# A two-layer streaming encoder: constants loaded later, attention probabilities and values as half-precision pairs, the norm's steps in another order

## The reference

```python
z = x @ w_in[l] + b_in[l]
...
kv = (ckv_all @ w_ukv[l]).reshape(B, past + T, MLA_HEADS, NOPE_DIM + V_DIM)
a_out = _mla_attention(qn, qr, positions, kv[..., :NOPE_DIM], kr_all, kv[..., NOPE_DIM:], kpos)
...
h, C, n, m = _mlstm(mq, mk, mv, mi, mf, C_init, n_init, m_init)
...
c_out, v_rows = _gmlp(gu, gv, gmlp_ln_g[l], gmlp_ln_b[l], gmlp_ws[l], gmlp_bs[l])
...
x = _layernorm(DN_ALPHA * x + merged @ w_out[l], ln1_g[l], ln1_b[l])
moe_out = _moe(x, router_w, router_b, moe_w_gate[l], moe_w_up[l], moe_w_down[l],
               shared_w_gate[l], shared_w_up[l], shared_w_down[l])
x = _layernorm(DN_ALPHA * x + moe_out, ln2_g[l], ln2_b[l])
```

```python
s = jnp.einsum('bqhd,bkhd->bhqk', qn, kn) + jnp.einsum('bqhd,bkd->bhqk', qr, kr)
...
p = jax.nn.softmax(s, axis=-1)
return jnp.einsum('bhqk,bkhd->bqhd', p.astype(v.dtype), v)
```

## Time and profile before

| | |
|---|---|
| median of 3 runs | 1021.45 us (1021.13 to 1022.71) |
| profiled execution, own time | 1021.76 us |
| its span, first to last instruction | 1019.9 us |
| PE busy | 979.0 us (96%) |
| PEld (weight loads, beside PE) | 757.6 us (74%) |
| DVE busy | 806.5 us (79%) |
| ACT busy | 655.3 us (64%) |
| DMA | 205.02 MB, mean 201 GB/s |
| mean granted TensorE clock | 0.993 of full |

### The profile page before, as it was taken

The page is one execution under the profiler, slowest core; times in us unless marked ns, Lnnn a source line. Parts: engine busy times, 40 slices in busy tenths (PEclk is TensorE's granted clock), DMA queues, the critical chain, the costliest instruction groups (busy, mean ns, idle before and its releaser), DMA issues.

```text
span 1019.9 us, 24037 instructions
## 1 busy us (share of the span) xinstructions
PE 979.0 (96%) x9862; PEld 757.6 (74%) x9862; DVE 806.5 (79%) x1436; ACT 655.3 (64%) x1057; POOL 0.7 (0%) x10
## 2 busy tenths in 40 slices
PE   8999999999999999999999999999999989999995
PEld 6877777777776799976568777777777768998653
DVE  4796767654689899998888876676448899999986
ACT  5675454754355799876776645556543659987864
POOL 0000000000000000000000000000000000000000
PEclk9999999999999999999999999999999999999998
DMA  9845454423465199998836534442334435999961
GB/s 352 301 170 166 148 151 121 131 83 110 145 222 166 54 322 368 360 361 317 288 125 210 181 124 141 151 146 85 104 124 148 144 102 167 359 364 365 375 233 55
DMA packets 59652, 205.02 MB, mean 201 GB/s; under 512 B 7216, under 2 KB 10348, under 8 KB 59020
## 3 DMA queue, kind: packets, MB, share of 16 engines
q1 hardware_dynamic: 55980, 195.95, 55.8%
q10 hardware_dynamic: 3552, 7.42, 2.1%
HBM read 198.76 MB, written 3.40 MB: 198 GB/s over the span
## 4 chain that ended last, share of the span: by engine, by line
PE 64%; DVE 21%; DVEq 5%; ACT 4%; issue 3%; DMA 1%; SPq 1%; ACTq 0%
PE bank L1777 37%; DVE wlo L1074 12%; PE bank L1801 4%; DVEq L1700 4%; PE bank L2313 3%; ACT whi L555 2%; PE bank L2145 2%; PE bank L1806 1%; PE bank L2000 1%; DMA w<-in_w 1%; DVE mo L1702 1%; PE bank L2034 1%; PE bank L2076 1%; DVE xT L1087 1%; PE bank L2329 1%
## 5 line engine op out<-in xcount | busy, mean ns | idle before, releaser
L1074 DVE SCALAR_TENSOR_TENSOR wlo<-w,whi 128x1024 f16<-128x1024 f32 x358 | 428.9, 1220 | 69.4 <-ACT whi L555 67.9
L555 ACT ACTIVATE whi<-w 128x1024 f16<-128x1024 f32 x358 | 368.8, 1048 | 81.6 <-PE bank L1777 48.1
L1777 PE MATMUL bank<-xhi,whi 128*128 128x320 f16 x688 | 206.2, 300 | 0.7 <-DVE wlo L1074 0.6
L1777 PE MATMUL bank<-xhi,wlo 128*128 128x320 f16 x688 | 205.7, 299 | 0.0
L1777 PE MATMUL bank<-xlo,whi 128*128 128x320 f16 x688 | 205.7, 299 | 0.0
L1777 PE MATMUL bank<-arena_b,whi 128*128 128x112 f16 x2048 | 161.7, 213 | 7.7 <-DVE wlo L1074 6.7
L1777 PEld LDWEIGHTS bank<-arena_b,whi 128*128 128x128 f16 x2048 | 149.5, 98 | 12.8 <-issue 8.6
L1777 PE MATMUL bank<-arena_b,wlo 128*128 128x112 f16 x1024 | 157.3, 213 | 0.0
L1777 PEld LDWEIGHTS bank<-arena_b,wlo 128*128 128x128 f16 x1024 | 100.1, 98 | 0.0
L1777 PEld LDWEIGHTS bank<-xhi,whi 128*128 128x128 f16 x688 | 67.2, 98 | 30.8 <-issue 2.8
L1777 PEld LDWEIGHTS bank<-xhi,wlo 128*128 128x128 f16 x688 | 67.3, 98 | 26.1
(11 more groups left out here) (378 smaller groups left out, 1747.4 us busy)
## 6 DMA issues: line engine op xcount, KB each, us to landing
w<-in_w SPq DMA_DIRECT2D x358, 512.0 KB, 4.9
arena_b<-head_rows ACTq DMA_DIRECT2D x2, 1920.0 KB, 7.3
xT<-in_x SPq DMA_DIRECT2D x2, 640.0 KB, 5.5
out_y<-xT SPq DMA_DIRECT2D x4, 320.0 KB
rows<-in_rows ACTq DMA_DIRECT2D x1, 1024.0 KB, 10.5
rows<-in_rows SPq DMA_DIRECT2D x1, 1024.0 KB, 5.9
out_ckv<-arena_a SPq DMA_DIRECT2D x2, 320.0 KB
acc<-kr SPq DMA_DIRECT2D x2, 288.0 KB
```

The lines of the kernel that those rows point to most:

```text
L555: A(whi[:, n % SLOTS, :], w32[:, n % RAW, :], ACT.Copy, scale=WS).then_inc(hi_done.sem, 1)
L1074: V.scalar_tensor_tensor(wlo[:, n % SLOTS, :], w32[:, n % RAW, :], WS, whi[:, n % SLOTS, :], ALU.mult, ALU.subtract).then_inc(lo_done.sem, 1)
L1777: ins = M(out, w[:, s, sub * P:(sub + 1) * P], rhs(part, k), start=(n == 0), stop=(n == 3 * len(subs) - 1))
```

## The change

**Start.** Four constants (`ident`, `scan_keep`, `m_init`, `mats16`) stay ahead of block 4. `front_load` (mask, cosine, sine and the head rows) follows block 8, `head_load` (the five tables that ScalarE issued) block 10, and `router_load` (router weights, selection tables and biases) a block of the heads. Two new signals, `tables_in` and `router_in`, are waited for where the tables are used. The exponentials of the head rows and their store stand one block earlier on ScalarE.

**Attention.** The values are kept as two f16 parts (`v_hl`: high by ScalarE, low by VectorE). The exponential is written to one buffer `prob`; ScalarE multiplies it by 4096 over the sum into a high f16 part, VectorE writes the low one (`probs_lo`). The transposes are f16 matmuls of both parts with an identity, six a unit. Their result is again split in two (`columns_hi`, `columns_lo`), and the values are three f16 products each in place of one f32. On TensorE a unit is now scores, filler, values of the unit two before, transposes of the unit before. ScalarE and VectorE take the columns of the unit two before at the start of a unit. The second half's keys are copied out in two parts around unit 2's exponentials, its queries stand in unit 1.

**Norms.** The base `acc` is filled chunk by chunk as each merged chunk has been split, and the router's high part before it. In the first norm the square of residual 6 is added before the last product is waited for, no longer behind residual 7. In `ln_vector` one chunk is centred before the variance and the other seven within the loop, with four drains in it instead of two.

The diff, cut; renamed waits and declarations are left out:

```diff
             sp.dma_start(par[:, :], d["par"]).then_inc(par_in.sem, 16)
-            for dst, name in ((ident[:, :], "ident"), (mmask[:, :], "mmask"),
-                              (scan_keep[:, :], "scan_keep"), (mats16[:, :, :], "mats16"),
...
+            for dst, name in ((ident[:, :], "ident"), (scan_keep[:, :], "scan_keep"), (m_init[:, :], "m_init"),
+                              (mats16[:, :, :], "mats16")):
                 sp.dma_start(dst, d[name]).then_inc(consts_in.sem, 16)
...
+                for dst, name in ((mmask[:, :], "mmask"), (cosT[:, :], "cos"), (sinT[:, :], "sin")):
+                    sp.dma_start(dst, d[name]).then_inc(tables_in.sem, 16)
+                sp.dma_start(rows[:, :], d["rows"][0:1, :].broadcast_to([P, 4 * GW])).then_inc(rows_fr.sem, 16)
...
+            def head_load():
+                for dst, src in ((cache, d["cache"][0:P, :]), (kr[:, 0:PAST], d["krope"][0:ROPE, :]),
...
+            def router_load():
...
+                if n == RAW:
+                    front_load()
+                if n == RAW + 2:
+                    head_load()
+                if n == M0 + RAW:
+                    router_load()
...
-                if l == 0:
-                    act.dma_start(rows[:, :], d["rows"][0:1, :].broadcast_to([P, 4 * GW])
-                                  ).then_inc(rows_fr.sem, 16)
-                for dst, src in () if l else ((cache, d["cache"][bass.ds(l * P, P), :]),
...
+                    if i == 1:
+                        act.wait_ge(r_arg.sem, r_arg.value(l, 1))
+                        A(r_x[:, 1:4, :], r_x[:, 1:4, :], ACT.Exp).then_inc(r_exp.sem, 1)
...
+                def k_out(hf, parts=range(4)):
+                    for n in parts:
...
                 def exps(u):
                     act.wait_ge(s_max.sem, s_max.value(l, u + 1))
+                    if u:
+                        act.wait_ge(p_lo.sem, p_lo.value(l, u))
...
+                def probs_hi(u):
+                    act.wait_ge(p_inv.sem, p_inv.value(l, u + 1))
                     if u >= 2:
...
+                        A(prob_h[:, u % 2, 0, 0:P], prob[:, 0:P], ACT.Copy, scale=sm[:, 6:7])
+                        A(prob_h[:, u % 2, 0, P:3 * P], prob[:, P:3 * P], ACT.Copy, scale=sm[:, 7:8]
+                          ).then_inc(p_hi.sem, 1)
...
+                def columns_hi(u):
...
+                        A(prob_t[:, u % 2, 0, :], bank[6][:, 0:3 * P], ACT.Copy).then_inc(t_hi.sem, 1)
...
-                    A(br_hi[:, p * T:(p + 1) * T], bank[7][:, 0:T], ACT.Copy, scale=XS
+                    A(br_hi[:, p * T:(p + 1) * T], bank[7][:, 0:T], ACT.Copy, scale=1 / PS
...
                 for u in range(UNITS):
+                    if u >= 2:
+                        columns_hi(u - 2)
+                    if u == 2:
+                        k_out(1, (0, 1))
...
+                    if u == 4:
+                        v_out_hi(1)
+                    elif u not in (2, 3):
+                        gate_tanh(FILLER[u - 1] if u else 2)
+                    exps(u)
                     if u == 2:
-                        q_out(1)
-                    elif u == 3:
-                        k_out(1)
-                    elif u != 4:
-                        gate_tanh(FILLER[u - 1] if u else 2)
-                    if u:
-                        probs_out(u - 1)
-                    exps(u)
+                        k_out(1, (2, 3))
                     if u != 3:
                         hi_a(FILLER[u])
+                    if u == 1:
+                        q_out(1)
+                    probs_hi(u)
+                columns_hi(UNITS - 2)
                 gate_tanh(13)
                 hi_a(14)
                 gate_tanh(14)
-                probs_out(UNITS - 1)
+                columns_hi(UNITS - 1)
...
+                act.wait_ge(router_in.sem, 16 * 6)
+                A(rw_hi[:, :, :], rw[:, :, :], ACT.Copy, scale=WS).then_inc(rw_h.sem, 1)
+                for c in range(KD):
+                    act.wait_ge(m_lo.sem, m_lo.value(l, c + 1))
+                    if l:
                         a = A(acc[:, c * T:(c + 1) * T], xT[:, c * T:(c + 1) * T], ACT.Identity,
...
-                else:
-                    A(acc[:, :], xT[:, :], ACT.Copy, scale=ALPHA).then_inc(acc_pre.sem, 1)
...
+                    else:
+                        a = A(acc[:, c * T:(c + 1) * T], xT[:, c * T:(c + 1) * T], ACT.Copy, scale=ALPHA)
+                a.then_inc(acc_pre.sem, 1)
...
-                for c in range(2):
-                    centred(c)
+                centred(0)
...
-                centred(2)
+                dve.drain()
                 dve.wait_ge(ln_std.sem, ln_std.value(l, k + 1))
                 for c in range(KD):
-                    if c in (2, 5):
+                    if c in (1, 3, 5, 7):
                         dve.drain()
                     scaled(c)
-                    if c + 3 < KD:
-                        centred(c + 3)
+                    for n in (1, 2) if c == 0 else (c + 2,) if c < 6 else ():
+                        centred(n)
...
-                if k == 0 and c > 1:
+                if k == 0 and 1 < c < KD - 1:
...
+                dve.wait_ge(tables_in.sem, 16 * 3)
...
+                def probs_lo(u):
+                    dve.wait_ge(p_hi.sem, p_hi.value(l, u + 1))
+                    if u % 3 < 2:
+                        V.scalar_tensor_tensor(prob_h[:, u % 2, 1, 0:P], prob[:, 0:P], sm[:, 6:7],
+                                               prob_h[:, u % 2, 0, 0:P], ALU.mult, ALU.subtract)
+                        V.scalar_tensor_tensor(prob_h[:, u % 2, 1, P:3 * P], prob[:, P:3 * P], sm[:, 7:8],
+                                               prob_h[:, u % 2, 0, P:3 * P], ALU.mult, ALU.subtract
+                                               ).then_inc(p_lo.sem, 1)
...
+                def columns_lo(u):
+                    dve.wait_ge(t_hi.sem, t_hi.value(l, u + 1))
+                    if u % 3 < 2:
+                        V.tensor_tensor(prob_t[:, u % 2, 1, :], bank[6][:, 0:3 * P], prob_t[:, u % 2, 0, :],
...
                 for u in range(UNITS):
+                    if u >= 2:
+                        columns_lo(u - 2)
...
+                    if u == 1:
+                        rotate(1)
+                    if u == 2:
+                        rotated(1)
                     dve.wait_ge(p_exp.sem, p_exp.value(l, u + 1))
...
-                    if w == 2:
-                        V.tensor_scalar(prob[:, u % 2, 0:P], prob[:, u % 2, 0:P], sm[:, 6:7], None,
-                                        ALU.mult)
...
+                    V.tensor_scalar(sm[:, 6:6 + w], sm[:, 6:6 + w], PS, None, ALU.mult
+                                    ).then_inc(p_inv.sem, 1)
                     if u != 3:
                         lo_a(FILLER[u])
+                    probs_lo(u)
+                columns_lo(UNITS - 2)
                 lo_a(14)
+                columns_lo(UNITS - 1)
                 lo_a(15)
...
                 def transposes(u):
...
+                        pe.wait_ge(t_lo.sem, t_lo.value(l, u))
...
                         n = P if u % 3 < 2 or i < 2 else TS
-                        a = TR(bank[6][0:n, i * P:(i + 1) * P], prob[:, u % 2, i * P:i * P + n],
...
+                        for y in range(2):
+                            a = M(bank[6][0:n, i * P:(i + 1) * P], prob_h[:, u % 2, y, i * P:i * P + n],
+                                  mats16[:, 0, :], start=(y == 0), stop=(y == 1))
...
+                    def weigh(out, kt, rows_, vc, at, first, last):
+                        for x, y in ((0, 0), (0, 1), (1, 0)):
+                            a = M(out, v_hl[0:rows_, hf, x, kt, vc], prob_t[0:rows_, u % 2, y, at],
+                                  start=(first and x == 0 and y == 0), stop=(last and x == 1))
...
-                            M(o[:, 0:P], v_kv[:, hf, 2, vc], prob_t[:, u % 2, 0, :], start=True, stop=True)
...
+                            weigh(o[:, 0:P], 2, P, vc, slice(0, P), True, True)
...
                 gate(2)
                 for u in range(UNITS):
                     scores(u)
-                    if u:
-                        transposes(u - 1)
-                    if u >= 2:
-                        values(u - 2)
...
                         gate(FILLER[u])
+                    if u >= 2:
+                        values(u - 2)
+                    if u:
+                        transposes(u - 1)
                 gate(14)
+                values(UNITS - 2)
                 transposes(UNITS - 1)
-                values(UNITS - 2)
                 gate(15)
                 values(UNITS - 1)
```

More of the change, by code:

```diff
@@ L63 @@
 GS = 1024.0
+PS = 4096.0
 BRANCHES = (1, 2, 0)
@@ L536, in _ @@
             nc.gpsimd.memset(gm16[:, :, :], 0.0).then_inc(consts_set.sem, 1)
-            for first in (num_ps, att_done, dc_ps, h_done, g_done, s_ps, sp_ps, o_lo, t_sb, stored, c_stored,
```

(17 more changed lines are left out.)

151 lines of the change are left out of this document (77 added, 74 removed).

## The result

The changed kernel takes 1022.51 us (median of 12 runs, 1021.88 to 1023.65), the kernel before, run beside it, 1020.46 (12 runs, 1018.69 to 1022.71): a ratio of 1.0021 with a 95% interval of 1.0013 to 1.0029. It is slower by 2 us, outside the range 1009.5 to 1019.5. The 12 runs of before lie 1 us under the three that the prediction was made against.

A forecast was written before the change was run, and what follows sets the result against it. The prediction took matmuls as 64% of the last chain, with VectorE's circle bounding the changed attention. Start -4.5, attention -2.8, norms +1.0 and +0.7 gave -5.6 us: 1015.8 as a median, eight-in-ten range 1009.5 to 1019.5.

The forecast's parts named there:

- Start, -4.5: Start: late constants remove TensorE's wait before its first token block, 2.7 us idle and 1.8 us slow clock.
- Attention, -1.4 a layer: Attention: steady units and tail gain, early units lose 1.1 us; net -1.4 us a layer, -2.8 in all.
- 14.7: Attention: TensorE's own time for three units after the change, 14.7 us against 16.12, 5.7 us a layer if nothing else is late.
- VectorE's circle of 15.1: Attention: VectorE's in-order chain with the added residuals takes 15.1 us for three units, more than TensorE's 14.7.
- the three waits of the early units: Attention: TensorE waits 1.3 us behind key copies, 0.4 for unit 0, and 1.0 to 1.3 at unit 3's columns; 3.0 together.
- Norm: the last, +1.0: Last norm: more subtractions and drains in VectorE's loop, all on the path to the last store, +1.0 us.
- The one that ends layer 0, +0.7: Norm ending layer 0: first part 0.43 us earlier, residual parts 0.7 later with TensorE already waiting, +0.7 us.
- The two first norms, 0 and 0: First norms: layer 0's later parts go unnoticed by slowed TensorE; layer 1's loop loss is offset by single residual parts; 0 each.
- D: Rival: the clock falls in the attention after waits of 1.3 us, costing up to 7 us, 1017.5 to 1023; chance 0.12.
- A: Rival: TensorE bounds the attention after all, -5.7 us a layer, 1007.2, or 1010 to 1013 in part; chance 0.17 together.
- C: Rival: attention's f16 matmuls do not hide their 98 ns weight loads, +4.3 us a layer, 1027; chance 0.05.
- B: Rival: at the start transfers hide nothing, TensorE still stands before its first token block, 1019 to 1020.5; chance 0.08.

The follow-up runs named there:

- null: The kernel before, run again with nothing changed and profiled separately: 1020.72 us, ratio 1.0008.
- att_pad: Kernel before with only the attention change, plus 64 always-satisfied waits in TensorE's untaken branch: 1022.63 us, ratio 1.0024.
- before_shift: Kernel before with 338 never-executed waits in TensorE's untaken branch, moving the jump's target: 1024.23 us, ratio 1.0036.
- late: Kernel before with only the late constants and the head rows' exponentials one block earlier: 1016.12 us, ratio 0.9967.
- after: The full changed kernel, against the kernel before: 1022.51 us, ratio 1.0021.
- two_products: Changed kernel with two of the three f16 products in the attention values, one left out: 1017.06 us, ratio 0.9968 to the kernel before.
- late_keys: Kernel before with late constants, attention and 64 dead waits; second half's keys copied as parts 0 to 2, then 3: 1015.95 us, ratio 0.9959.
- late_norm: Kernel before with only the late constants and the norm's other order: 1019.69 us, ratio 0.9996.
- after_pad: Changed kernel with 64 never-executed waits in TensorE's untaken branch: 1019.82 us, ratio 0.9989 to the kernel before.
- A and B: Parts of the change, not rivals, in phrases about kernels: the first is the late constants, the second the attention change; no single time.
- abc: Changed kernel with the norm's old order put back: 1020.20 us, ratio 0.9997 to the kernel before.
- combined: Kernel before with late constants, single residual parts, attention with keys copied as parts 0 to 2 then 3, and 64 dead waits: 1015.80 us, ratio 0.9959.

## Why the prediction was wrong

**Start, -4.5: right in the trace** (-4.67 against null; the gap, the first block and its tail as forecast). Against the median it gave 3.4 (2.1 to 4.6). In part this was luck: the 1.8 for the clock was read from one execution, and the traces of att_pad and before_shift have the wait without the slow clock. Their attention starts no earlier for it, because TensorE then waits at the heads for the gate chain, of which the prediction said "nothing waits for it". late has no such wait, and is 5.7 and 4.9 ahead of them.

**Attention, -1.4 a layer: wrong, +0.3.** The main step that failed is TensorE's account, "14.7" for three units. Two of them in after, each with its values, transposes, scores and gate block:

```profile
220.20 1.09 PE L2148 MATMUL bank<-ysq,arena_b 128*64 128x64 f16 x18
221.23 0.51 PE L2132 MATMUL bank<-mats,mu_var 128*128 128x128 f16 x6
221.67 0.77 PE L2121 MATMUL bank<-arena_c,arena_b 98*64 98x256 f32 x8
222.38 0.31 PE L1857 MATMUL bank<-xhi,whi 128*128 128x320 f16 x1
...
225.74 0.69 PE L2148 MATMUL bank<-ysq,arena_b 128*64 128x128 f16 x9
226.36 0.51 PE L2132 MATMUL bank<-mats,mu_var 128*128 128x128 f16 x6
226.71 0.87 PE L2114 MATMUL bank<-arena_c,arena_b 98*128 98x128 f32 x4
227.42 0.30 PE L1857 MATMUL bank<-xhi,whi 128*128 128x320 f16 x1
```

From start to start nine value matmuls take 0.62 (forecast 0.50) and eighteen 1.03 (0.75), six transposes 0.35 to 0.56 (0.34). Three units, from the gate block at 217.01 to that at 232.87, take 15.86, against 16.11 before. TensorE's work in the stage, 78.03 less 1.40 of waits, is 76.6, against 77.7: 1.1 less, where 5.7 was forecast. The price of one more matmul, 0.056, was right (two_products: 0.057). What was left out is what does not count by matmuls: 0.11 and 0.43 in the values, up to 0.2 in the transposes, and 0.1 between a gate block and the values. Over three units the values are 0.52 over their forecast, the transposes 0.33, the step from gate block to values 0.18 and the scores 0.15: 1.2 together, which is the difference between 14.7 and 15.86. The price of 0.056 was taken from a run of 48 of one kind, and used for runs of 6 to 18 between matmuls of other kinds. The Trainium skill (TensorE: Matmul & The Clock Gate, Back-to-back issue gap) gives 81 ns for a load and matmul pair at 128 columns. The nine come to 69 each and the transposes to 58 to 93, so as a mean over short runs its figure is nearer than the 56 that was taken, and as the price of one more pair it is not.

What was said to be late next was not. VectorE's circle of 15.1 for three units was never the bound, because TensorE itself needed 15.86. Of the three waits of the early units two exist, 0.93 (forecast 1.3; its cause shown by late_keys) and 0.47 (forecast 1.0 to 1.3; its cause not tested), 1.40 instead of 3.0:

```profile
209.90 0.66 PE L2148 MATMUL bank<-ysq,arena_b 128*64 128x128 f16 x9 [0.47 <-DVE br_lo L1495]
```

So -1.1 + 1.4 = +0.3. The 1.3 came from a sum given as 6.6; the terms named for it (3.4, 1.0, 1.2, 0.65, 0.9) come to 7.15, and with them the wait would have been put at 1.8, further off still.

**Norm: the last, +1.0, right** for the norm itself (3.41 at its end less 2.45 at its first sum, late_norm against late); 0.3 of a delay that comes in is taken up in the experts, so the table shows 0.7. **The one that ends layer 0, +0.7: 1.1.** **The two first norms, 0 and 0: 0.8 each.** The step that failed is "which its slowed TensorE does not notice". The TensorE of that one execution was slowed by the clock; in null and late_norm it was not, and then each low part that comes later is waited for. In layer 1 the forecast let the single residual parts pay for the loop; they do give 0.6, but they belong to another part. Together the order costs 3.4 in the trace and 3.6 in the medians, where 1.7 was forecast.

**Not in the sum at all: the gap behind the jump.** It gives 2.7 by the medians of after and after_pad, 1.9 by their traces at layer 1's token blocks: the gap, and the slow clock behind it. Part of both is hidden in after_pad by waits for VectorE's low parts.

**The baseline.** The prediction took 1021.76, its trace's own time, as 0.3 over the median. With more runs it is 1.3 over it, since it holds a slow clock in the first norm (1.2), which only two of the nine traces with the old order of the norm have (before and att_pad). Against the time of null's profiled execution, 1020.4, the terms as traced are -4.7 for the start, +0.6 for the attention, +3.4 for the norms, -0.6 for the residual parts and +1.9 for the gap, +0.6 in all. The two traces differ by 1.7, the medians by 2.1. Of the 1.1 between sum and traces, 0.4 is the slow clock that after has in the first norm of layer 0, and 0.4 a wait of VectorE at the second norm's sum with nothing that it waits for. The six kernels with both A and B have it (after, after_pad, abc, two_products, late_keys, combined); att_pad, with B alone, and the kernels with A alone do not:

```profile
499.80 0.49 DVE L1176 TENSOR_TENSOR mu_var<-mu_var,acc 128x320 f32<-128x320 f32 x1 [0.45 <-issue]
```

The last 0.3 was not traced. 10 of after's 12 runs have a mean granted clock of 0.992 or 0.993, all of after_pad's 0.995 or 0.996, which speaks for a slow clock behind the gap in most executions, not in the profiled one alone.

The rivals: D, a clock that falls, was given 0.12 and put into the attention, where the clock stayed whole. It fell in the norms and behind the gap. A had it right that TensorE is the bound of the steady units, but its gain was the account that failed. C had the right direction and the wrong reason: the 54 matmuls of three units take 3.6 us, 0.067 each, above the 0.056 forecast and below C's 0.084, but one more costs 0.057 and not the 0.098 of a load that is not hidden. B did not come: there is no wait before the first token block.

## What to carry to other kernels

Price short runs of matmuls by rows of short runs: the rate of a long one holds for one more matmul, not for the changes between kinds, and here they took four fifths of the promised gain. A term of zero that rests on a slow neighbour must be looked at in a second execution, since the neighbour's slowness may be the chance of one trace. And where a change lengthens an engine's program ahead of a jump, compare with a kernel whose dead code is padded, or the code's place is measured together with the edit.

## What the runs showed of the hardware

- In after, abc and before_shift TensorE stood 1.8 to 2.7 us with nothing that the profile shows ("issue"), before the 8th matmul behind a jump. Dead code of 64 waits moved it away in one kernel, and 338 made it in another. Each gap ended 2.2 to 2.8 us behind one 16.4 KB packet of the instruction queue, so it is most likely a wait for instructions.
- The granted clock fell to 0.50 behind waits of TensorE of 1.56 to 2.88 us, seen in two or three of the table's windows of 2.5 us, in the start, after the gap, and in one norm or another. Waits of the same length had it in one execution and not in another: in the first norm of layer 0 before (1.86) and null (1.87), 1.21 us between them, and at the start null (2.88) and att_pad (2.87).
- In runs of six and nine, one more f16 matmul with a new stationary part of 64 columns costs 0.057 us at 128 moving columns, in runs of 12 and 18 0.033 at 64, beside 0.11 and 0.43 us for the run.
- VectorE too stood 0.45 us with nothing that the profile shows, at one place of the six kernels with A and B.
